# A pair of up blocks by Strassen's scheme: seven quarter products for eight in two feed-forward stages

## The chip, the cores and the metric

The kernel runs on one core of one Trainium2 chip. The metric is the time of one execution on the device in microseconds (us). Arrays are fp32; the kernel was timed in three runs, and one more execution was profiled.

## The reference

A sequence of 512 tokens of 1024 features passes through four pairs of mixer and feed-forward stage. The last two feed-forward stages are plain ones:

```python
def sqrelu_mlp(h, w1, w2):
    return jnp.square(jax.nn.relu(h @ w1)) @ w2
...
x = x + sqrelu_mlp(rms_norm_2(x, norm_ffn[i]), ffn_w1[i], ffn_w2[i]).astype(x.dtype)
```

Here `ffn_w1` is 1024 x 4096 (up) and `ffn_w2` is 4096 x 1024 (down). The change is in `h @ w1` of these two stages.

## The kernel before

**Layout.** Everything is held feature by feature: a tile has 128 features on the partitions and 512 tokens beside each other. x has 8 such tiles (`KT`), the hidden layer of a plain stage has 32 (`MLP_TILES`). All weights are one stream of blocks of 128 x 1024 words (`BLOCK`), consumed in the order of `STREAM`. An up block holds, for 128 hidden features, the 8 weight squares of 128 x 128 along the 1024 input features; a down block holds the 8 squares along the 1024 output features.

**Split in two parts.** A product of fp32 precision is made of three matmuls on rounded operands (type fp32r). Each weight block is split by ScalarE into a high part (`act_split`, L300, `wraw` to `whi`) and by VectorE into the low rest (`dve_split`, L323, `wlo` = `wraw` - `whi`). The normalised x has `hnhi` and `hnlo`, a hidden tile has `ahi` (L559) and `alo` (L564). `three` (L341 to L343) issues high x high, high x low, low x high into one PSUM bank. `wlo` lies in the same memory as `wraw`; there are four slots.

**A plain up stage.** `pe_up` takes one block after the other: 8 x 3 matmuls of 512 columns into bank m % 4; the first two are interleaved with the making of `hnhi` and `hnlo` (`pe_up_first`). The norm's factor `rstd` is computed meanwhile: squares on ScalarE (L397), added up by VectorE (L409), summed over the features by a matmul with ones (L419), then Ln and Exp on ScalarE (L361, L362). It multiplies each token's column after the product: VectorE makes relu times `rstd` (L849) into the hidden tile in `arena`, ScalarE squares it (L834). After each block `w_used` is raised; block i is loaded when block i - 4 has been used (`sp_stream`). The loops run on the engines, four blocks a trip (`tiles`).

**A plain down stage.** All 8 banks accumulate over the 32 hidden tiles; `dve_add` (L750) adds them to x as they are finished. `BANKS_FREED` gives the order in which the first tile's products go to the banks, and `MIXERS` what each bank waits for.

**Order.** Each engine runs its own list of instructions in order, and semaphores (`wait_ge`, `then_inc`) order the engines. Before the change the work of GpSimd is in other stages; in its list a load of tables waits for the first mixer of the plain part and is issued near the start of the first plain feed-forward stage.

## Time and profile before

| | |
|---|---|
| time, median of 3 runs | 2635.78 us (2635.65 to 2636.78) |
| the profiled execution's own time | 2636.36 us |
| its span in the trace | 2634.6 us |
| mean granted clock of TensorE | 1.0 (2.4 GHz) |
| TensorE busy | 2604.4 us (99%) |
| VectorE, ScalarE, GpSimd busy | 1526.8, 1178.7, 249.9 us |

The span goes from the first to the last instruction; the time of an execution has some 1.8 us around it. The duration of a matmul in the trace contains its way through the array, so matmuls overlap in time; the distance between the starts of two is what one costs in a stream. PE is TensorE, PEld its weight loads, DVE VectorE, ACT ScalarE, POOL GpSimd, SP the queue that loads the weights.

### The profile page before, as it was taken

How to read it: one execution, taken by the hardware profiler on the slowest of the kernel's cores; microseconds unless marked ns; L12 is line 12 of the kernel's file. 1: busy time of each engine (PE TensorE's matmuls, PEld its weight loads, DVE VectorE, ACT ScalarE, POOL GpSimd, SP SyncE). 2: the span in 40 equal slices, each digit the busy share in tenths (PEclk: the TensorE clock that was granted, in tenths of full speed). 3: DMA queues.
4: the chain of work that ended last, by engine and by line, in shares of the span. 5: the costliest groups of instructions: out<-in, count | busy, mean ns of one | idle time of the engine just before them, and what ended most of it. 6: DMA issues, size and time to landing. Idle time of an engine off the chain costs nothing. (4 is left out here: it accounts for less than half of the span.)

```text
span 2634.6 us, 33003 instructions
## 1 busy us (share of the span) xinstructions
PE 2604.4 (99%) x11682; PEld 2021.1 (77%) x11682; DVE 1526.8 (58%) x2136; ACT 1178.7 (45%) x1858; POOL 249.9 (9%) x204
## 2 busy tenths in 40 slices
PE   9999999999999999999999999999999999999999
PEld 7855788888786557788888776788888777888887
DVE  4466677643988785677643787543333536533333
ACT  3326544333547894444333687532333425422332
POOL 0021100000104781100000130000000002000000
PEclk9999999999999999999999999999999999999999
DMA  5310333233244442233333220233333321233332
GB/s 212 96 56 9 102 96 96 96 96 96 86 132 127 122 128 80 80 97 99 98 96 96 94 64 1 75 100 96 97 99 98 104 81 53 92 96 97 99 98 96
DMA packets 71430, 246.02 MB, mean 93 GB/s; under 512 B 7564, under 2 KB 7692, under 8 KB 70960
## 3 DMA queue, kind: packets, MB, share of 16 engines
q1 hardware_dynamic: 70256, 236.43, 28.9%
q0 software_dynamic: 944, 8.46, 0.9%
q8 instruction: 51, 0.84, 0.1%
q14 instruction: 35, 0.29, 0.0%
q10 hardware_dynamic: 144, 0.00, 0.0%
HBM read 242.63 MB, written 2.24 MB: 93 GB/s over the span
## 5 line engine op out<-in xcount | busy, mean ns | idle before, releaser
L323 DVE TENSOR_TENSOR wlo<-wraw,whi 128x1024 fp32r<-128x1024 f32 x405 | 506.4, 1251 | 574.3 <-ACT whi L300 573.5
L341 PE MATMUL bank<-hnhi,whi 128*128 128x512 f32 x1952 | 779.0, 399 | 2.0 <-DVE arena L1567 1.2
L342 PE MATMUL bank<-hnlo,whi 128*128 128x512 f32 x1952 | 760.6, 390 | 0.0
L343 PE MATMUL bank<-hnhi,wlo 128*128 128x512 f32 x1952 | 760.4, 390 | 0.0
L300 ACT ACTIVATE whi<-wraw 128x1024 fp32r<-128x1024 f32 x409 | 430.3, 1054 | 537.4 <-DMA wraw<-in_w 537.2
L341 PE MATMUL bank<-ahi,whi 128*128 128x512 f32 x1184 | 463.1, 391 | 1.0 <-DVE alo L564 0.7
L342 PE MATMUL bank<-alo,whi 128*128 128x512 f32 x1184 | 460.8, 389 | 0.0
L343 PE MATMUL bank<-ahi,wlo 128*128 128x512 f32 x1184 | 460.7, 389 | 0.0
L341 PEld LDWEIGHTS bank<-hnhi,whi 128*128 128x128 f32 x1952 | 366.4, 188 | 110.1 <-issue 34.4
L342 PEld LDWEIGHTS bank<-hnlo,whi 128*128 128x128 f32 x1952 | 366.6, 188 | 80.5 <-issue 6.5
L343 PEld LDWEIGHTS bank<-hnhi,wlo 128*128 128x128 f32 x1952 | 366.4, 188 | 77.8
L341 PEld LDWEIGHTS bank<-ahi,whi 128*128 128x128 f32 x1184 | 222.2, 188 | 51.4 <-DVE alo L564 3.8
L343 PEld LDWEIGHTS bank<-ahi,wlo 128*128 128x128 f32 x1184 | 222.2, 188 | 46.4
L342 PEld LDWEIGHTS bank<-alo,whi 128*128 128x128 f32 x1184 | 222.3, 188 | 46.1 <-issue 0.5
L785 ACT ACTIVATE mT<-mT,cols 128x512 f32<-128x512 f32 x88 | 71.8, 816 | 221.0 <-DVE mT L483 221.0
L834 ACT ACTIVATE arena<-arena (+1 forms) x64 | 40.4, 632 | 221.7 <-DVE arena L849 221.7
L559 ACT ACTIVATE ahi<-arena 128x512 fp32r (+1 forms) x140 | 88.2, 631 | 97.1 <-PE bank L343 96.4
L808 DVE SCALAR_TENSOR_TENSOR mT<-mT,cols 128x511 f32<-128x511 f32 x88 | 66.1, 751 | 97.3 <-ACT mT L785 97.3
L564 DVE TENSOR_TENSOR alo<-arena,ahi 128x512 fp32r<-128x512 f32 x140 | 96.8, 691 | 36.4 <-ACT ahi L559 34.1
L744 POOL TENSOR_TENSOR xT<-xT,mT 128x512 f32<-128x512 f32 x20 | 33.9, 1728 | 873.3 <-DVE mT L736 873.3
L483 DVE TENSOR_TENSOR arena<-bank,rstd 128x512 f32<-128x512 f32 (+3 forms) x48 | 36.6, 765 | 116.0 <-PE bank L343 104.5
L849 DVE SCALAR_TENSOR_TENSOR arena<-bank,rstd 128x512 f32 (+1 forms) x64 | 44.1, 691 | 102.9 <-PE bank L343 96.4
(306 smaller groups left out, 2511.1 us busy)
## 6 DMA issues: line engine op xcount, KB each, us to landing
wraw<-in_w SPq DMA_DIRECT2D x410, 512.0 KB, 3.6
arena<-cs_scratch SPq DMA_DIRECT2D x20, 512.0 KB, 6.0
over_a<-cs_scratch SPq DMA_DIRECT2D x12, 512.0 KB, 6.0
arena<-in_rpb POOLq DMA_DIRECT2D x1, 2880.0 KB, 14.2
out_dram<-xT SPq DMA_DIRECT2D x8, 256.0 KB, 2.0
arena<-in_t_step POOLq DMA_DIRECT2D x2, 897.0 KB, 4.8
arena<-in_t_ab POOLq DMA_DIRECT2D x1, 1536.0 KB, 6.8
xT<-in_x SPq DMA_DIRECT2D x2, 512.0 KB, 5.9
```

What stands on the lines that cost most here:

```text
L300: act.activation(whi[:, slot * BLOCK:(slot + 1) * BLOCK], wraw[:, slot * BLOCK:(slot + 1) * BLOCK], ACT.Copy).then_inc(sem("w_hi"), 1)
L323: dve.tensor_tensor(wlo[:, slot * BLOCK:(slot + 1) * BLOCK], wraw[:, slot * BLOCK:(slot + 1) * BLOCK], whi[:, slot * BLOCK:(slot + 1) * BL ...
L341: pe.matmul(out, wh, ah, start=start, stop=False)
L342: pe.matmul(out, wh, al, start=False, stop=False)
L343: return pe.matmul(out, wl, ah, start=False, stop=stop)
L483: dve.tensor_tensor(out, src, by, ALU.mult).then_inc(sem(done), 1)
L559: act.activation(ahi[:, c:c + SEQ], src(k), ACT.Copy).then_inc(sem("a_hi"), 1)
L564: dve.tensor_tensor(alo[:, c:c + SEQ], MIXERS[name][0](k), ahi[:, c:c + SEQ], ALU.subtract).then_inc(sem("a_lo"), 1)
L785: act.activation(cbuf(m), ubuf(m), ACT.Identity, bias=col("fb", m + 44 * f), scale=col("fw", m + (132 * f + 44))).then_inc(sem("ffn_center ...
L808: dve.scalar_tensor_tensor(out=c[:, 1:SEQ], in0=u[:, 0:SEQ - 1], scalar=col("fw", m + 132 * f), in1=c[:, 1:SEQ], op0=ALU.mult, op1=ALU.add ...
L834: act.activation(tile(m), tile(m), ACT.Square).then_inc(sem("mlp_hidden"), 1)
L849: dve.scalar_tensor_tensor(out=tile(m), in0=bank[m.base % 4][:, :], scalar=0.0, in1=rstd[:, :], op0=ALU.max, op1=ALU.mult).then_inc(sem("m ...
```

## The change

In both plain stages blocks 0 to 7 stay as they were (their order written out, no loop). From block 8 on two blocks are one product: 256 hidden features x 1024 inputs x 512 tokens, cut in half each way, is a 2 x 2 product of quarters. It is done with seven quarter products (Winograd's form of Strassen's scheme) with 15 sums in place of eight products:

- Weights: a11, a12 are the two halves of the first block's inputs, a21, a22 of the second's. GpSimd makes s1 = a21 + a22, s2 = s1 - a11, s3 = a11 - a21, s4 = a12 - s2, each 128 x 512. ScalarE and VectorE split each of a11, s1, a12, s2, a22, s3, s4 in high and low (`high`, `low`): seven pieces of 512 columns where two of 1024 were.
- Tokens: t1 to t4 are sums of quarters of the normalised x (inputs in halves, tokens in halves). They are made once per stage, during blocks 0 to 7, by GpSimd (t1) and VectorE (t2, t3, t4), with high and low parts (`tok_hi`, `tok_lo`).
- Products: each is 4 x 3 matmuls of 256 columns (`product`). Three banks per pair, x, w and z, two pairs in turn. x starts with a11; ScalarE copies x to z (`copy_z`); a12 is added to x, s2 and then s3 to z. w takes s1; ScalarE copies it to SBUF (`copy_w`), VectorE writes w = z + copy (`sum_w`) before s3 and s4 are added, and after s3 writes the fourth quarter z + copy to the hidden tile (`sum_c`); a22 is then added to z. VectorE makes relu times `rstd` in four pieces of 256 columns.
- TensorE's order in cycle n: a11(n), s3(n-1), s4(n-1), s1(n), a22(n-1), a12(n), s2(n). The products of a pair run over two cycles.
- The high parts have one place each in `whi` (a22 has two), the low parts one each. A load of a block of pair n + 2 waits for the split of a12(n) and for s4(n).
- The load of tables on GpSimd's queue moves behind the first stage's pairs; the first down product visits banks 6 and 7 first.

```diff
+PAIRS = (MLP_TILES - PLAIN) // 2
+QUARTER = 4 * P
 WIDE = 897
 NEG = -1e30
...
 
+        def extra(b):
+
+            return 5 * PAIRS * sum(b >= FIRST[f"mlp_down{f}"] for f in range(2))
...
             rows = FIRST["c_in"] + 17
-            for lo, hi in ((4, rows), (rows, Z0 + 5), (Z0 + 5, Z0 + 18), (Z0 + 18, NBLOCKS)):
...
                         sp_rows(sp, i.base - lo)
+            for f in range(2):
+                sp_pairs(sp, f)
+                rest = FIRST[f"mlp_down{f}"] + 4
+                for i in tiles(sp, rest, NBLOCKS if f else FIRST["mlp_up1"] + PLAIN + 4):
+                    sp.wait_ge(sem("w_used"), i.value(1, extra(rest) - 3))
...
             slot = i.base % 4
-            dve.wait_ge(sem("w_hi"), i.value(1, 1))
...
+        USED = pair_counts([s for c in range(PAIRS + 1) for s in before(
+            ("a11", c), ("s3", c - 1), ("s4", c - 1), ("s1", c), ("a22", c - 1), ("a12", c), ("s2", c))])
+        SPLIT = pair_counts(before(("a11", 0), ("s1", 0), ("a12", 0), ("s2", 0), ("a22", 0)) + [
+            s for c in range(PAIRS) for s in before(("a11", c + 1), ("s3", c), ("s4", c), ("s1", c + 1), ("a22", c + 1),
+                                                    ("a12", c + 1), ("s2", c + 1))])
...
+        def quarter_hi(f, q, n):
+
+            freed, half = {"a11": (4, 0), "s1": (4, 1), "a12": (5, 0), "s2": (5, 1), "s3": (6, 0), "s4": (6, 1),
+                           "a22": (7, n % 2)}[q]
+            a = (FIRST[f"mlp_up{f}"] + freed) % 4 * BLOCK + half * QUARTER
+            return whi[:, a:a + QUARTER]
...
+        def sp_pairs(sp, f):
+
+            for i in range(first_pair(f) + 4, FIRST[f"mlp_down{f}"] + 4):
+                n = (i - first_pair(f)) // 2 - 2
+                sp.wait_ge(sem("w_lo"), split(f, "a12" if n else "a22", n))
+                sp.wait_ge(sem("sum_pool"), pool_summed(f, "s4", n))
+                sp_load(sp, At(i))
+
+        def pool_pairs(pool, f):
...
+            for n in range(PAIRS):
+                wait_block(pool, f, n, 0)
+                wait_block(pool, f, n, 1)
+                if n:
+                    pool.wait_ge(sem("w_lo"), split(f, "s1", n - 1))
+                pool.tensor_tensor(sum_raw("s1"), block_raw(f, n, "a21"), block_raw(f, n, "a22"), ALU.add)\
+                    .then_inc(sem("sum_pool"), 1)
+                if n:
+                    pool.wait_ge(sem("w_lo"), split(f, "s2", n - 1))
+                pool.wait_ge(sem("sum_pool"), pool_summed(f, "s1", n))
+                pool.tensor_tensor(sum_raw("s2"), sum_raw("s1"), block_raw(f, n, "a11"), ALU.subtract)\
+                    .then_inc(sem("sum_pool"), 1)
+                if n:
+                    pool.wait_ge(sem("w_lo"), split(f, "s3", n - 1))
+                pool.tensor_tensor(sum_raw("s3"), block_raw(f, n, "a11"), block_raw(f, n, "a21"), ALU.subtract)\
+                    .then_inc(sem("sum_pool"), 1)
+                if n:
+                    pool.wait_ge(sem("w_lo"), split(f, "s4", n - 1))
+                pool.wait_ge(sem("sum_pool"), pool_summed(f, "s2", n))
+                pool.tensor_tensor(sum_raw("s4"), block_raw(f, n, "a12"), sum_raw("s2"), ALU.subtract)\
+                    .then_inc(sem("sum_pool"), 1)
+
...
+            def high(q, n):
+
+                if n == 0 or (q, n) == ("a22", 1):
+                    act.wait_ge(sem("w_used"), plain_used(f, {"a11": 4, "s1": 4, "a12": 5, "s2": 5, "s3": 6, "s4": 6, "a22": 7}[q]))
+                else:
+                    act.wait_ge(sem("w_used"), used(f, q, n - 2 if q == "a22" else n - 1))
+                if q in SUM_AT:
+                    act.wait_ge(sem("sum_pool"), pool_summed(f, q, n))
+                    src = sum_raw(q)
+                else:
+                    wait_block(act, f, n, q == "a22")
+                    src = block_raw(f, n, q)
+                act.activation(quarter_hi(f, q, n), src, ACT.Copy).then_inc(sem("w_hi"), 1)
+
+            def copy_z(n):
+                act.wait_ge(sem("w_used"), used(f, "a11", n))
+                if n == 0:
+                    act.wait_ge(sem("mlp_relu"), relu_done(f, 6))
+                if n >= 2:
+                    act.wait_ge(sem("mlp_relu"), relu_done(f, PLAIN + 2 * (n - 2) + 1))
+                act.activation(pair_bank(n, "z"), pair_bank(n, "x"), ACT.Copy).then_inc(sem("sum_copied"), 1)
+
+            def copy_w(n):
+                act.wait_ge(sem("w_used"), used(f, "s1", n))
+                if n >= 2:
+                    act.wait_ge(sem("sum_dve"), c_summed(f, n - 2))
+                act.activation(w_copy(n), pair_bank(n, "w"), ACT.Copy).then_inc(sem("sum_copied"), 1)
...
+                    for j in range(KT):
+                        act_square(act, j)
+                    act_split(act, At(FIRST[name] + 3))
+                    for j in range(4):
+                        ins = act.activation(over_a[:, j * SEQ:(j + 1) * SEQ], xt(j), ACT.Copy, scale=col(g, g0 + j))
+                    ins.then_inc(sem("sum_copied"), 1)
+                    act_norm_rstd(act, norm)
+                elif m <= 5:
...
+            for n in range(PAIRS):
+                copy_z(n)
+                if n == 0:
+                    high("a22", 0)
+                if n + 1 < PAIRS:
+                    high("a11", n + 1)
+                high("s3", n)
+                high("s4", n)
+                copy_w(n)
+                if n + 1 < PAIRS:
+                    high("s1", n + 1)
+                if n:
+                    hidden_square(PLAIN + 2 * (n - 1))
+                if n + 1 < PAIRS:
+                    high("a22", n + 1)
+                    high("a12", n + 1)
+                if n:
+                    hidden_square(PLAIN + 2 * (n - 1) + 1)
+                if n + 1 < PAIRS:
+                    high("s2", n + 1)
+            act.wait_ge(sem("w_used"), used(f, "s1", PAIRS - 1))
+            act_split(act, At(FIRST[f"mlp_down{f}"]))
+            act.wait_ge(sem("w_lo"), split(f, "s4", PAIRS - 1))
+            act_high(act, f"mlp_down{f}", At(0))
+            act_high(act, f"mlp_down{f}", At(1))
+            act.wait_ge(sem("w_used"), used(f, "s2", PAIRS - 1))
+            act_split(act, At(FIRST[f"mlp_down{f}"] + 1))
+            hidden_square(MLP_TILES - 2)
+            hidden_square(MLP_TILES - 1)
+            act.wait_ge(sem("w_used"), used(f, "a22", PAIRS - 1))
+
...
+            def low(q, n):
+                dve.wait_ge(sem("w_hi"), split(f, q, n))
+                src = sum_raw(q) if q in SUM_AT else block_raw(f, n, q)
+                dve.tensor_tensor(quarter_low(q, n), src, quarter_hi(f, q, n), ALU.subtract).then_inc(sem("w_lo"), 1)
+
+            def sum_w(n):
+                dve.wait_ge(sem("w_used"), used(f, "s2", n))
+                dve.wait_ge(sem("sum_copied"), w_copied(f, n))
+                dve.tensor_tensor(pair_bank(n, "w"), pair_bank(n, "z"), w_copy(n), ALU.add).then_inc(sem("sum_dve"), 1)
+
+            def sum_c(n):
+                dve.wait_ge(sem("w_used"), used(f, "s3", n))
+                dve.tensor_tensor(pair_tile(n, 1, 1), pair_bank(n, "z"), w_copy(n), ALU.add).then_inc(sem("sum_dve"), 1)
+
+            def relu_z(n):
+                dve.wait_ge(sem("sum_dve"), c_summed(f, n))
+                relu(pair_tile(n, 1, 1), pair_tile(n, 1, 1), 1)
+                dve.wait_ge(sem("w_used"), used(f, "s4", n))
+                relu(pair_tile(n, 0, 1), pair_bank(n, "w"), 1).then_inc(sem("mlp_relu"), 1)
...
+            for n in range(PAIRS):
+                if n:
+                    sum_w(n - 1)
+                else:
+                    low("a22", 0)
+                if n + 1 < PAIRS:
+                    low("a11", n + 1)
+                if n:
+                    sum_c(n - 1)
+                low("s3", n)
+                if n:
+                    relu_z(n - 1)
+                low("s4", n)
+                if n + 1 < PAIRS:
+                    low("s1", n + 1)
+                if n:
+                    dve.wait_ge(sem("w_used"), used(f, "a22", n - 1))
+                    relu(pair_tile(n - 1, 1, 0), pair_bank(n - 1, "z"), 0).then_inc(sem("mlp_relu"), 1)
+                if n + 1 < PAIRS:
+                    low("a22", n + 1)
+                dve.wait_ge(sem("w_used"), used(f, "a12", n))
+                relu(pair_tile(n, 0, 0), pair_bank(n, "x"), 0)
+                if n + 1 < PAIRS:
+                    low("a12", n + 1)
+                    low("s2", n + 1)
+            dve_split(dve, At(FIRST[f"mlp_down{f}"]))
+            dve_low_part(dve, f"mlp_down{f}", At(0))
+            sum_w(PAIRS - 1)
+            dve_low_part(dve, f"mlp_down{f}", At(1))
+            sum_c(PAIRS - 1)
+            dve_split(dve, At(FIRST[f"mlp_down{f}"] + 1))
+            relu_z(PAIRS - 1)
+            dve.wait_ge(sem("w_used"), used(f, "a22", PAIRS - 1))
+            relu(pair_tile(PAIRS - 1, 1, 0), pair_bank(PAIRS - 1, "z"), 0).then_inc(sem("mlp_relu"), 1)
+
...
+            def product(q, n, c, start=False):
+
+                pe.wait_ge(sem("w_lo"), split(f, q, n))
+                out, hi, lo = pair_bank(n, c), quarter_hi(f, q, n), quarter_low(q, n)
+                t = {"s1": "t1", "s2": "t2", "s3": "t3", "a22": "t4"}.get(q)
+                if t and n == 0:
+                    pe.wait_ge(sem("sum_dve"), token_low(f, t))
+                for j in range(4):
+                    if t:
+                        ah, al = tok_hi[:, token(t, j)], tok_lo[:, token(t, j)]
                     else:
+                        half = slice(HALF_N, SEQ) if q == "s4" else slice(0, HALF_N)
+                        ah, al = (a[:, half] for a in hn_parts(j if q == "a11" else 4 + j))
+                    wh, wl = hi[:, j * P:(j + 1) * P], lo[:, j * P:(j + 1) * P]
+                    if start:
+                        mm = three(pe, out, (wh, wl), (ah, al), j == 0, j == 3)
                     else:
+                        pe.matmul(out, wh, ah, start=False, stop=False, skip_group_check=True)
+                        pe.matmul(out, wh, al, start=False, stop=False, skip_group_check=True)
+                        mm = pe.matmul(out, wl, ah, start=False, stop=j == 3, skip_group_check=True)
+                mm.then_inc(sem("w_used"), 1)
+
+            for n in range(PAIRS + 1):
+                if n < PAIRS:
+                    pe.wait_ge(sem("mlp_relu"), relu_done(f, (4, 7)[n] if n < 2 else PLAIN + 2 * (n - 2)))
+                    product("a11", n, "x", True)
+                if n:
+                    pe.wait_ge(sem("sum_dve"), w_summed(f, n - 1))
+                    product("s3", n - 1, "z")
+                    product("s4", n - 1, "w")
+                if n < PAIRS:
+                    if n == 0:
+                        pe.wait_ge(sem("mlp_relu"), relu_done(f, 5))
+                    product("s1", n, "w", True)
+                if n:
+                    pe.wait_ge(sem("sum_dve"), c_summed(f, n - 1))
+                    product("a22", n - 1, "z")
+                if n < PAIRS:
+                    pe.wait_ge(sem("sum_copied"), z_copied(f, n))
...
+        def pair_banks(total):
+            def free(pe, m):
+                if m < 6:
+                    pe.wait_ge(sem("mlp_relu"), total - {0: 2, 1: 2, 2: 2, 3: 1, 4: 1, 5: 0}[m])
+            return free
+
...
                 .then_inc(sem("tables_loaded"), 16)
             pool_mla(pool)
-            pool.wait_ge(sem("x_ready"), 40)
+            pool_pairs(pool, 0)
+            pool.wait_ge(sem("w_used"), used(0, "a22", PAIRS - 1))
             pool.dma_start(arena[:, ML_T["stepF"]:ML_T["stepF"] + TABLE_WORDS["step"]], A["t_step"])\
                 .then_inc(sem("tables_loaded"), 16)
             pool_ml(pool)
+            pool_pairs(pool, 1)
```

## Rows read from the trace of the kernel before

**Rows 1.** The page's header and busy times of the engines.
```profile
span 2634.6 us, 33003 instructions
PE 2604.4 (99%) x11682; PEld 2021.1 (77%) x11682; DVE 1526.8 (58%) x2136; ACT 1178.7 (45%) x1858; POOL 249.9 (9%) x204
```

**Rows 2.** Stretches: plain blocks 0 to 7, then the rest of each up stage.
```profile
core 0: us, PE busy (x) PEld busy (x) DVE busy (x) ACT busy (x) POOL busy (x), PEclk, DMA share, GB/s
1705.00:1749.00 44.00, 44.00 (x193) 36.06 (x193) 24.09 (x30) 20.24 (x29) 0.56 (x1) 1.00 0.40 129
1750.00:1880.00 130.00, 130.00 (x575) 107.67 (x574) 47.24 (x50) 38.97 (x50) 0.00 (x0) 1.00 0.32 97
2325.00:2456.00 131.00, 131.00 (x579) 108.48 (x578) 47.24 (x50) 38.97 (x50) 0.00 (x0) 1.00 0.31 96
```

**Rows 3.** Timeline of one up block: start us, us, engine, line.
```profile
1783.11 0.69 DVE L849 SCALAR_TENSOR_TENSOR arena<-bank,rstd 128x512 f32 x1 [1.75 <-PE bank L343]
...
1783.25 0.39 PE L343 MATMUL bank<-hnhi,wlo 128*128 128x512 f32 x1
1783.26 0.19 PEld L341 LDWEIGHTS bank<-hnhi,whi 128*128 128x128 f32 x1
...
1784.46 1.04 ACT L300 ACTIVATE whi<-wraw 128x1024 fp32r<-128x1024 f32 x1
...
1785.54 1.23 DVE L323 TENSOR_TENSOR wlo<-wraw,whi 128x1024 fp32r<-128x1024 f32 x1 [1.74 <-ACT whi L300]
...
1788.55 0.69 DVE L849 SCALAR_TENSOR_TENSOR arena<-bank,rstd 128x512 f32 x1 [1.78 <-PE bank L343]
```

**Rows 4.** Timeline of TensorE: runs of short plain fp32 matmuls.
```profile
1090.87 2.32 PE L701 MATMUL bank<-base_t 128*128 128x256 f32 x10
...
2230.22 0.60 PE L2564 MATMUL bank<-arena,mT 128*128 128x128 f32 x4
```

**Rows 5.** Timeline of weight loads, whose matmuls have two columns.
```profile
1515.21 0.86 PEld L2097 LDWEIGHTS bank<-arena,over_hn 128*128 128x128 f32 x7 [0.24 <-issue]
```

**Rows 6.** Groups by shape: count, busy us, mean ns.
```profile
L564 DVE TENSOR_TENSOR alo<-arena,ahi 128x512 fp32r<-128x512 f32 x140 | 96.8, 691 | 36.4 <-ACT ahi L559 34.1
L2715 DVE SCALAR_TENSOR_TENSOR arena<-bank,arena 128x256 f32<-128x256 f32 x4 | 1.7, 417 | 0.7 <-PE bank L2589 0.7
L559 ACT ACTIVATE ahi<-arena 128x512 fp32r x88 | 55.8, 634 | 65.0 <-PE bank L343 64.4 <-DVE arena L1825 0.5
L954 ACT ACTIVATE arena<-bank 128x256 f32<-128x256 f32 x8 | 3.0, 379 | 0.2 <-PE bank L918 0.2
L701 PE MATMUL bank<-base_t 128*128 128x256 f32 x40 | 9.3, 379 | 0.0
L2564 PE MATMUL bank<-arena,mT 128*128 128x128 f32 x16 | 2.4, 274 | 0.0
L1646 POOL TENSOR_TENSOR mT<-arena 128x512 f32<-128x512 f32 x40 | 50.4, 1287 | 68.9 <-DVE arena L1560 64.9 <-DMA arena<-cs_scratch 2.0 <-issue 1.9
```

**Rows 7.** Timeline: GpSimd beside VectorE, VectorE alone, the last matmul.
```profile
1464.76 6.78 POOL L744 TENSOR_TENSOR xT<-xT,mT 128x512 f32<-128x512 f32 x4 [359.20 <-DVE mT L736]
...
1465.85 1.12 DVE L402 SCALAR_TENSOR_TENSOR hnlo<-xT,cols,hnhi 128x512 fp32r<-128x512 f32 x1
...
2277.82 0.69 DVE L750 TENSOR_TENSOR xT<-xT,bank 128x512 f32<-128x512 f32 x1
2278.43 0.75 DVE L402 SCALAR_TENSOR_TENSOR hnlo<-xT,cols,hnhi 128x512 fp32r<-128x512 f32 x1
...
2630.74 1.36 DVE L750 TENSOR_TENSOR xT<-xT,bank 128x512 f32<-128x512 f32 x2
...
2631.00 0.39 PE L343 MATMUL bank<-ahi,wlo 128*128 128x512 f32 x1
```

**Rows 8.** Timeline: TensorE restarts after a wait for VectorE.
```profile
2230.42 0.69 DVE L2702 TENSOR_TENSOR arena<-bank,rstd 128x512 f32<-128x512 f32 x1 [2.52 <-PE bank L343]
...
2231.22 0.19 PEld L341 LDWEIGHTS bank<-hnhi,whi 128*128 128x128 f32 x1 [0.37 <-issue]
...
2231.26 0.47 PE L341 MATMUL bank<-hnhi,whi 128*128 128x512 f32 x1 [0.21 <-DVE arena L2702]
2231.56 0.40 PE L342 MATMUL bank<-hnlo,whi 128*128 128x512 f32 x1
...
2232.26 0.39 PE L342 MATMUL bank<-hnlo,whi 128*128 128x512 f32 x1
```

**Rows 9.** DMA issues with us to landing, and ScalarE's wait for the norm sum.
```profile
wraw<-in_w SPq DMA_DIRECT2D x410, 512.0 KB, 3.6
arena<-in_t_step POOLq DMA_DIRECT2D x2, 897.0 KB, 4.8
...
L361 ACT ACTIVATE rstd<-bank,stats 128x512 f32<-128x512 f32 x1 | 0.7, 690 | 5.5 <-PE bank L419 5.5
```

More of the change, by code:

```diff
@@ L48 @@
 MLP_TILES = 4 * DM // P
+PLAIN = 8
+PAIRS = (MLP_TILES - PLAIN) // 2
+QUARTER = 4 * P
 WIDE = 897
@@ L273, in sp_stream @@
             rows = FIRST["c_in"] + 17
-            for lo, hi in ((4, rows), (rows, Z0 + 5), (Z0 + 5, Z0 + 18), (Z0 + 18, NBLOCKS)):
+            for lo, hi in ((4, rows), (rows, Z0 + 5), (Z0 + 5, Z0 + 18), (Z0 + 18, FIRST["mlp_up0"] + PLAIN + 4)):
                 if lo == rows:
@@ L852, in pe_mlp_up, with pair_counts, before @@
-        def pe_mlp_up(pe, f, norm):
-            pe_up(pe, f"mlp_up{f}", norm, [(2, 4, None, 0), (4, 32, "mlp_relu", 32 * f - 3)])
+        def pair_counts(order):
+            return {q: i + 1 for i, q in enumerate(order)}
+        def before(*steps):
+            return [(q, n) for q, n in steps if 0 <= n < PAIRS]
+        USED = pair_counts([s for c in range(PAIRS + 1) for s in before(
+            ("a11", c), ("s3", c - 1), ("s4", c - 1), ("s1", c), ("a22", c - 1), ("a12", c), ("s2", c))])
@@ new lines, in quarter_low, with pair_bank, pair_tile, w_copy @@
+        def quarter_low(q, n):
+            if q == "a22" and n % 2:
+                return odd_lo[:, :]
+            a = ("a11", "s1", "a12", "s2", "s3", "s4", "a22").index(q) * QUARTER
+            return quarter_lo[:, a:a + QUARTER]
+        def pair_bank(n, c):
+            return bank[3 * (n % 2) + "xwz".index(c)][:, 0:HALF_N]
+        def pair_tile(n, second, half):
+            return tile(PLAIN + 2 * n + second)[:, half * HALF_N:(half + 1) * HALF_N]
+        def w_copy(n):
+            return sq[:, n % 2 * HALF_N:(n % 2 + 1) * HALF_N]
```

185 lines of the change are left out of this document (149 added, 36 removed).

## The prediction

> **What bounds the kernel now.** I read the page's busy shares first: TensorE is busy for 99% of the span, VectorE for 58%, ScalarE for 45%, GpSimd for 9% [rows 1]. The table of stretches says the same of both feed-forward up stages: TensorE 130 us in 130 us at the full granted clock, VectorE 36%, ScalarE 30%, GpSimd idle [rows 2]. So the time of an up block is its column work. In the timeline the same VectorE instruction (L849, one per block) starts at 1783.11 and 1788.55 [rows 3], and a block has 8 x 3 products: 5.44/24 = 0.2267 us from one 128x512 product to the next. Each has a weight load of 0.19 us beside it [rows 3]. At 2.4 GHz 512 columns are 0.2133 us, so 0.0133 us is something else; on it the change hangs.
>
> **What the change does to TensorE.** Blocks 8 to 31 of a stage become 12 pairs, in two stages 24 pairs. A pair was 48 products of 512 columns, 48 x 0.2267 = 10.88 us; 24 pairs are 261.1 us. It becomes 7 quarter products of 4 x 3 = 12 matmuls of 256 columns: 84 matmuls, with 84 weight loads where there were 48. The columns streamed fall by an eighth, weight loads rise by three quarters. Break-even for the bare stream is 10.88/84 = 0.1295 us per matmul.
>
> No row shows a 256-column matmul on data rounded for one pass. The nearest are:
> - Plain fp32 matmuls take twice as long per column: ten of 256 columns take 2.32 us in all with one lasting 0.379, so (2.32 - 0.38)/9 = 0.216 apart; four of 128 columns with weights of their own are (0.60 - 0.27)/3 = 0.110 apart (runs [rows 4], one matmul's duration [rows 6]). The second streams as long as our case (0.1067 us), with a new 128x128 weight load each. So load and stream do overlap at this length: lower bound 0.110.
> - Two-column matmuls show the bare cost of loads: seven in 0.86 us, (0.86 - 0.19)/6 = 0.112 [rows 5].
> - The 0.0133 us over the columns is either per matmul, giving 0.1067 + 0.0133 = 0.120, or per column (a sixteenth), giving 0.1133. For plain fp32 the surplus is some 0.0025 at 128 and 256 columns alike [rows 4], thus per matmul.
> - From above: bare load plus surplus, 0.112 + 0.013 = 0.125; and, if the slower steps after a restart (2231.56 to 2232.26 in three steps, 0.233 each [rows 8]) never ended, 0.1067 + 0.020 = 0.127.
>
> I take 0.120, since the only surplus seen at two lengths is per matmul. 2016 matmuls are 241.9 us: 19.2 below 261.1. The ends are 0.110 (221.8) and 0.127 (256.0).
>
> The Trainium skill (TensorE: Matmul & The Clock Gate, Back-to-back issue gap) says that in a stream of weight loads and matmuls both set the spacing, and gives 81 ns at 128 columns against 56 without loads, which speaks against this change. An estimate from that page, 0.025 us on top of 0.109, would be 0.134 and 2016 x 0.134 = 270 us; rows 4 show no such surplus for plain fp32.
>
> **The wait that the new order puts in.** TensorE goes a11(n+1), s3(n), s4(n), s1(n+1), a22(n), a12(n+1), s2(n+1). s3(n) waits for `sum_w(n)`, which needs s2(n), the product just before a11(n+1); so one quarter product, 12 x 0.120 = 1.44 us, covers it. But VectorE's list has `low("s2", n+1)` ahead of `sum_w(n)`, and that waits for ScalarE's `high("s2", n+1)`, which waits for s2(n) to leave its single place in `whi`. From the time at which a11(n+1) issues:
> - last matmul of s2(n) drains: modelled duration less pitch, 0.389 - 0.227 = 0.16; the waiting engine starts 0.02 after (matmul over at 2631.39, the second of the two L750 begins at 2632.10 - 0.69 = 2631.41) [rows 7]: 0.18
> - high, 128x512 copy by ScalarE: 0.63; handover 0.04 (L300 ends at 1785.50, L323 starts at 1785.54) [rows 3, 6]
> - low, 128x512 by VectorE: 0.69; sum_w, 256 columns with a PSUM operand: 0.42, starting some 0.08 before the one ahead is over, as L750 and L402 do (2278.43 - 2277.82 = 0.61 for 0.69), so 0.34 [rows 6, 7]
> - VectorE to TensorE: L2702 ends at 2231.11, the load starts at 2231.22, its matmul at 2231.26 and lasts 0.47 for 0.39: 0.11 + 0.04 + 0.08 = 0.23 [rows 8].
>
> 0.18 + 0.63 + 0.04 + 0.69 + 0.34 + 0.23 = 2.11 us. TensorE stands 2.11 - 1.44 = 0.67 us per cycle. Cycles 2 to 11 in two stages: 20 x 0.67 = 13.4 us. A steady cycle is 72 matmuls plus 2.11, 10.75 us for 10.88 before: the drop in columns pays for this wait and hardly more.
>
> **The two ends.** First cycle: the second weight block of pair 1 is issued as plain block 7 ends and lands 3.6 us later [rows 9]; then GpSimd's s1 and s2 at 1.28 each (the rows' solo value [rows 6]), high 0.63, low 0.69, sum_w 0.42 and handovers 0.3: 8.3 us, against 5 quarter products, 7.2: 1.1 us, twice. Last cycle: no a11 covers s3(11), and VectorE first does `dve_split` and `dve_low_part` of the down stage, 1.23 + 0.69 [rows 3, 6], after a12(11)'s relu of 0.42: done 2.5 us after a12 ends, with s2 lasting 1.44: 1.06 + 0.42 + 0.16 = 1.64 us, twice. Of the down stage only the first matmuls are moved; their first two banks (6 and 7) wait for nothing, and the others come 1.4 us and more later, after the last relus.
>
> **What lies beside.** Per pair VectorE has 7 lows at 0.69 and 6 operations of 256 columns at 0.42, 7.3 us; ScalarE 7 highs at 0.63, 2 PSUM copies at 0.38 and 2 squares at 0.63, 6.4; GpSimd 4 sums at 1.28, 5.1 [rows 6]. In 10.75 us all fit. I followed the order through one cycle: a12's high, the square and s2's high need 1.3 of the 1.44 us that s2 lasts, VectorE reaches `low("s2")` some 0.3 us early. The other waits of TensorE (`sum_c` for a22, `copy_z` for a12) have two or more products as cover. Weight loads of later pairs wait for GpSimd's s4 and a12's low, come some 0.5 us into the cycle before and are used after 8.8 us. In the plain blocks the work on tokens (4 ScalarE copies of 512, 4 roundings of 1024 columns, 12 VectorE instructions of 256, 4 of 1024, GpSimd's t1) adds 6.7 us to ScalarE's 20.2 and 9.9 to VectorE's 24.1 in a stretch of 44 us; the 2.5 us of copies ahead of `rstd` fall into ScalarE's wait of 5.5 us for the norm sum [rows 2, 9]; uncovered they would cost 2.5 us per stage, but bank 0 is next needed only at block 4. The table load on GpSimd's queue, moved behind the pairs, lands in 4.8 us [rows 9], and its tables are needed only by the mixer after the down stage of 32 x 5.44 = 174 us: nothing.
>
> GpSimd's sums read SBUF while VectorE's lows read two operands there. Where both ran, VectorE's L402 took 1.12 for 0.75 and GpSimd's sums 1.7 (four in 6.78 us) for 1.28 [rows 6, 7]. Per pair 10.3 us of such work share 10.75. `low("s2")` falls between GpSimd's s1(n+2) and s2(n+2), and slack of 0.3 us absorbs one collision of 0.4 nearly; I take nothing, and 0.4 x 20 = 8 us as the upper bound. The Trainium skill (SBUF — State Buffer, Who interferes with whom) says the later of the two blocks until the first ends. By that rule a low can be late by a whole sum; L402's 0.37 is well below that, so the trace agrees on the conflict and not on its size.
>
> **Sum.** 241.9 + 13.4 + 2.2 + 3.3 = 260.8 against 261.1: -0.3 us on the profiled execution's 2636.36 (span 2634.6 and 1.8 around it). That execution lies 0.6 above the median 2635.78, so on the median 2635.5 us.
>
> **Rivals.**
> 1. The surplus is per column or vanishes (0.110 to 0.115). At 0.1133: 228.4; cover 1.36, wait 0.75 x 20 = 15.0; ends 5.7: 249.1, 12 us less, 2624. At 0.110: 221.8 + 15.8 + 5.9 = 243.5, 2618. For it: 0.0133/0.2133 is exactly a sixteenth. Against: the fp32 rows.
> 2. The other side: weight loads, now as long as the stream, slow it. It decides above 0.123. At 0.125: 252.0 + 0.61 x 20 + 5.2 = 269.4, 2644; at 0.127: 256.0 + 0.59 x 20 + 5.1 = 272.9, 2648. For it: load floor 0.112 against a stream of 0.107. Against: 0.110 at 128 fp32 columns.
> 3. The shared SBUF reads of VectorE and GpSimd lengthen the chain by 0.4 per cycle: 2643.5.
> 4. Loads and matmuls do not overlap for rounded data: 0.107 + 0.112 = 0.219, 2016 x 0.219 = 441.5, over 2800. The 0.19 us loads in 0.227 us steps speak against it.
>
> **Chances.** Forecast (0.117 to 0.123, wait as above) 0.30; rival 1 0.34; rival 2 0.24; rival 3 0.09; rival 4 0.03. They spread: I can't tell fixed from proportional surplus by the trace. 0.2% or 5.3 us is about what a measurement of this kernel can tell from no change. Faster 0.35, same 0.30, slower 0.35. The range runs from 0.110 to 0.125 with one collision of 0.4 in every cycle (2644 + 8): 2619 to 2652; the likeliest case's own is 2630 to 2641.
>
> **What would show it.** In the changed profile: the step from one 256-column matmul to the next (0.120); TensorE idle once per pair ahead of the first matmul of s3, released by VectorE's `sum_w`, 0.67 us; 10.75 us from one pair's a11 to the next; VectorE about 68% busy there and its lows at 0.69 or up to 1.1. The prediction is wrong if the step is not 0.120 (each nanosecond is 1.8 us), if the wait before s3 is absent, or if TensorE waits at other products, for GpSimd or a weight block.

## The result

The changed kernel takes 2653.46 us (median of 4, 2653.11 to 2654.83), the kernel before beside it 2636.28 (4 runs, 2635.65 to 2637.04): a ratio of 1.0065, 95% interval 1.0054 to 1.0077. It is slower by 17 us and lies above the range of 2619 to 2652. The span went from 2634.6 [rows 1] to 2653.0 us. The page of the changed kernel, its header and busy times:

```profile
span 2653.0 us, 35180 instructions
PE 2595.4 (98%) x12546; PEld 2052.5 (77%) x12546; DVE 1684.5 (63%) x2384; ACT 1257.7 (47%) x2042; POOL 387.4 (15%) x302
```

TensorE is busy for 9 us less in a span that is 18 us longer, so it waits more than was forecast. The table of stretches shows where (its columns as in [rows 2]; the first two rows are the first wait and what follows it, the last two the two pair stretches):

```profile
1757.60:1763.90 6.30, 0.34 (x4) 0.14 (x2) 6.30 (x8) 1.26 (x3) 5.07 (x4) 0.88 0.07 16
1763.90:1768.00 4.10, 4.10 (x19) 4.10 (x20) 2.40 (x3) 0.63 (x1) 0.93 (x1) 0.50 0.66 251
1768.00:1876.00 108.00, 101.86 (x825) 99.83 (x825) 92.62 (x128) 58.93 (x108) 50.37 (x38) 0.99 0.26 92
1750.60:1890.40 139.80, 126.24 (x1009) 123.81 (x1008) 115.99 (x158) 72.15 (x132) 59.50 (x44) 0.98 0.26 95
2336.00:2475.00 139.00, 125.44 (x1008) 123.01 (x1008) 116.34 (x158) 72.20 (x132) 59.71 (x44) 0.98 0.27 96
```

A pair stretch (first matmul of the first pair to first matmul of the down stage) was 12 x 10.88 = 130.6 us; it is now 139.9 in the first stage and 139.2 in the second, 18.0 us more in all, of the 18.4 us by which the spans differ. The other 0.4 us lie ahead of the first stage. VectorE is busy for 116 of 140 us there, 83% where the prediction said 68%. In the first row VectorE is busy for all 6.30 us and TensorE for 0.34; in the second the granted clock is 0.50.

One line of the table of waits holds what is new in TensorE's waiting (engine and line waited for: us in all, times, longest):

```profile
PE bank L1201 <- DVE bank L1110: 27.1, 24, 6.0
```

L1110 is `sum_w`. So the place was forecast, once per pair ahead of s3; the size was not. TensorE's timeline has the wait in the first cycle and what follows it, and the wait in a steady cycle with the stream on both sides:

```profile
1757.64 0.28 PE L360 MATMUL bank<-hnhi,quarter_lo 128*128 128x256 f32 x1
1763.88 0.58 PE L1201 MATMUL bank<-tok_hi,whi 128*128 128x256 f32 x1 [5.96 <-DVE bank L1110]
1764.26 0.42 PE L1202 MATMUL bank<-tok_lo,whi 128*128 128x256 f32 x1
1764.47 0.41 PE L1203 MATMUL bank<-tok_hi,quarter_lo 128*128 128x256 f32 x1
...
1768.95 0.40 PE L1203 MATMUL bank<-hnhi,quarter_lo 128*128 128x256 f32 x1
...
1786.83 0.28 PE L359 MATMUL bank<-hnlo,whi 128*128 128x256 f32 x1
1786.95 0.28 PE L360 MATMUL bank<-hnhi,quarter_lo 128*128 128x256 f32 x1
1787.91 0.39 PE L1201 MATMUL bank<-tok_hi,whi 128*128 128x256 f32 x1 [0.68 <-DVE bank L1110]
1788.13 0.28 PE L1202 MATMUL bank<-tok_lo,whi 128*128 128x256 f32 x1
1788.25 0.29 PE L1203 MATMUL bank<-tok_hi,quarter_lo 128*128 128x256 f32 x1
```

The step from one matmul to the next is 0.12 us, as forecast. The distance over a steady wait is 1787.91 - 1786.95 = 0.96, over the first 1763.88 - 1757.64 = 6.24. After the first the steps are (1768.95 - 1764.26)/22 = 0.213 us, which is 256 columns at 1.2 GHz.

Why `sum_w` is late is in VectorE's and GpSimd's timelines of the same cycle. VectorE:

```profile
1782.44 1.51 DVE L1105 TENSOR_TENSOR quarter_lo<-over_a,whi 128x512 fp32r<-128x512 f32 x1 [0.42 <-ACT whi L997]
1783.88 0.41 DVE L1075 SCALAR_TENSOR_TENSOR arena<-bank,rstd 128x256 f32<-128x256 f32 x1
1784.21 1.76 DVE L1105 TENSOR_TENSOR odd_lo<-wraw,whi 128x512 fp32r<-128x512 f32 x1
1785.90 0.41 DVE L1075 SCALAR_TENSOR_TENSOR arena<-bank,rstd 128x256 f32<-128x256 f32 x1
1786.23 0.68 DVE L1105 TENSOR_TENSOR quarter_lo<-wraw,whi 128x512 fp32r<-128x512 f32 x1
1786.83 0.68 DVE L1105 TENSOR_TENSOR quarter_lo<-over_a,whi 128x512 fp32r<-128x512 f32 x1
1787.43 0.42 DVE L1110 TENSOR_TENSOR bank<-bank,sq 128x256 f32<-128x256 f32 x1
```

GpSimd and, below it, ScalarE's high part of s2 (L997) in that cycle:

```profile
1782.10 1.30 POOL L967 TENSOR_TENSOR over_a<-wraw,over_a 128x512 f32<-128x512 f32 x1 [0.63 <-DVE quarter_lo L1105]
1784.13 1.30 POOL L953 TENSOR_TENSOR over_a<-wraw 128x512 f32<-128x512 f32 x1 [0.72 <-DVE quarter_lo L1105]
...
1785.83 0.63 ACT L997 ACTIVATE whi<-over_a 128x512 fp32r<-128x512 f32 x1 [0.28 <-PE bank L1203]
```

The low of a22 (`odd_lo`) begins at 1784.21, 0.08 after GpSimd's sum, and is over at 1785.97, 0.54 after the sum's end at 1785.43: it takes 1.76 us for 0.69 [rows 6]. ScalarE hands over s2's high part at 1786.46; VectorE, which should have stood waiting for it, begins the low at 1786.83, 0.33 us late (0.04 is the handover). That is 0.96 instead of 0.63. The relus, with one operand in a PSUM bank, keep their 0.41 beside the same sums.

This is not one unlucky row. In the trace of the changed kernel 91 of the 168 lows begin while a GpSimd sum is under way, between 0.03 and 1.08 us after its start, and all 91 end 0.54 to 0.55 us after the end of that sum. The 75 lows that meet no sum take 0.67 to 0.69 us. So a low that meets a sum waits for the sum's end, and its length tells only how early in the sum it began.

In the first cycle the same happens to a whole row of lows. VectorE, then GpSimd:

```profile
1753.14 1.29 DVE L1105 TENSOR_TENSOR quarter_lo<-wraw,whi 128x512 fp32r<-128x512 f32 x2 [0.48 <-ACT whi L997]
1754.35 5.19 DVE L1105 TENSOR_TENSOR quarter_lo<-over_a,whi 128x512 fp32r<-128x512 f32 x3
1759.46 1.75 DVE L1105 TENSOR_TENSOR odd_lo<-wraw,whi 128x512 fp32r<-128x512 f32 x1
1761.13 0.41 DVE L1075 SCALAR_TENSOR_TENSOR arena<-bank,rstd 128x256 f32<-128x256 f32 x1
1761.46 1.41 DVE L1105 TENSOR_TENSOR quarter_lo<-wraw,whi 128x512 fp32r<-128x512 f32 x1
1762.80 0.68 DVE L1105 TENSOR_TENSOR quarter_lo<-over_a,whi 128x512 fp32r<-128x512 f32 x1
1763.40 0.42 DVE L1110 TENSOR_TENSOR bank<-bank,sq 128x256 f32<-128x256 f32 x1
```

```profile
1754.31 1.29 POOL L953 TENSOR_TENSOR over_a<-wraw 128x512 f32<-128x512 f32 x1 [4.69 <-DMA wraw<-in_w]
1755.75 1.56 POOL L958 TENSOR_TENSOR over_a<-over_a,wraw 128x512 f32<-128x512 f32 x1
1757.28 1.71 POOL L962 TENSOR_TENSOR over_a<-wraw 128x512 f32<-128x512 f32 x1
1758.95 1.71 POOL L967 TENSOR_TENSOR over_a<-wraw,over_a 128x512 f32<-128x512 f32 x1
1760.62 1.71 POOL L953 TENSOR_TENSOR over_a<-wraw 128x512 f32<-128x512 f32 x1
```

The weight block of pair 1 lands, and GpSimd runs five sums one behind the other. VectorE is never idle from 1753.14 to `sum_w` at 1763.40. From 1754.35 on it works through six lows and one relu in 9.05 us; alone they would take 6 x 0.61 + 0.34 = 4.0, counted from start to start. The longest of these lows takes 1.81 us.

### The profile page after: what moved, and what is told of

Same layout as the page of the kernel before. It is cut to its first block and busy times, and to the rows that moved or that the text cites. A ratio compares the mean times of both kernels' runs of the same rounds, so it can differ in the third digit from the quotient of the medians.

```text
span 2653.0 us, 35180 instructions
## 1 busy us (share of the span) xinstructions
PE 2595.4 (98%) x12546; PEld 2052.5 (77%) x12546; DVE 1684.5 (63%) x2384; ACT 1257.7 (47%) x2042; POOL 387.4 (15%) x302
## 5 line engine op out<-in xcount | busy, mean ns | idle before, releaser
L340 DVE TENSOR_TENSOR wlo<-wraw,whi 128x1024 fp32r<-128x1024 f32 x357 | 447.0, 1254 | 436.9 <-ACT whi L317 435.9
L358 PE MATMUL bank<-hnhi,whi 128*128 128x512 f32 (+1 forms) x1664 | 656.8, 395 | 2.0 <-DVE arena L1938 1.2
L359 PE MATMUL bank<-hnlo,whi 128*128 128x512 f32 (+1 forms) x1664 | 638.4, 384 | 0.0
L360 PE MATMUL bank<-hnhi,wlo 128*128 128x512 f32 x1568 | 611.1, 390 | 0.0
L317 ACT ACTIVATE whi<-wraw 128x1024 fp32r<-128x1024 f32 x361 | 380.0, 1055 | 479.7 <-DMA wraw<-in_w 479.4
L358 PEld LDWEIGHTS bank<-hnhi,whi 128*128 128x128 f32 x1664 | 312.8, 188 | 95.0 <-issue 34.5
L359 PEld LDWEIGHTS bank<-hnlo,whi 128*128 128x128 f32 x1664 | 313.0, 188 | 65.9 <-issue 6.5
L360 PEld LDWEIGHTS bank<-hnhi,wlo 128*128 128x128 f32 x1568 | 294.4, 188 | 62.7
L761 POOL TENSOR_TENSOR xT<-xT,mT 128x512 f32<-128x512 f32 x20 | 33.9, 1730 | 873.3 <-DVE mT L753 873.3
L1105 DVE TENSOR_TENSOR quarter_lo<-over_a,whi 128x512 fp32r<-128x512 f32 x96 | 99.9, 1044 | 19.1 <-ACT whi L997 17.5
L1201 PE MATMUL bank<-tok_hi,whi 128*128 128x256 f32 x288 | 85.1, 296 | 27.1 <-DVE bank L1110 27.1
```

The lines of the kernel that those rows point to most:

```text
L317: act.activation(whi[:, slot * BLOCK:(slot + 1) * BLOCK], wraw[:, slot * BLOCK:(slot + 1) * BLOCK], ACT.Copy).then_inc(sem("w_hi"), 1)
L340: dve.tensor_tensor(wlo[:, slot * BLOCK:(slot + 1) * BLOCK], wraw[:, slot * BLOCK:(slot + 1) * BLOCK], whi[:, slot * BLOCK:(slot + 1) * BL ...
L358: pe.matmul(out, wh, ah, start=start, stop=False)
L359: pe.matmul(out, wh, al, start=False, stop=False)
L360: return pe.matmul(out, wl, ah, start=False, stop=stop)
L1105: dve.tensor_tensor(quarter_low(q, n), src, quarter_hi(f, q, n), ALU.subtract).then_inc(sem("w_lo"), 1)
```

## The experiments

Eleven kernels ran, in three rounds and on two chips; all ratios are to the kernel before on the same chip and in the same round (2636.65 to 2637.03 us). Where a distance is given, it is from TensorE's last matmul before the wait to the first behind it. Theory: collisions of VectorE's lows with GpSimd's sums. Rivals: the order of `low("s2")` and `sum_w` alone, or something that the step of the matmul hides.

**1. Order: `sum_w(n)` ahead of `low("s2", n + 1)`.**

```diff
-                if n:
-                    sum_w(n - 1)
-                else:
+                if n == 0:
                     low("a22", 0)
...
                 if n + 1 < PAIRS:
                     low("a12", n + 1)
+                    sum_w(n)
                     low("s2", n + 1)
```

> The changed kernel with one swap on VectorE: sum_w(n) ahead of low of s2(n+1). Theory A (the order of VectorE's list makes the wait before s3): in the steady cycles TensorE's wait before s3 vanishes, because drain, sum_w and handover are some 0.8 us against 1.44 us of cover. 16 waits of 0.95 and 4 of 0.62 us go, 17.6 us, and 0.6 us in each first cycle: 2635 us, from 2653.5. The long wait in each first cycle stays, at some 5.6 us. Theory B (VectorE is late because its lows collide with GpSimd's sums, whatever the order): the waits move to other products and the time stays above 2642 us.

Measured: 2644.07 us (2642.47 to 2645.24), ratio 1.0026 (1.0016 to 1.0036). It gives back 9.4 of the 17 us and no more. The table counts the wait for `sum_w` 12 times in place of 24 (between those stand distances of some 0.36), and the mean of VectorE's lows (the group by shape below it: count, busy us, mean ns) is no better:

```profile
PE bank L1200 <- DVE bank L1110: 16.5, 12, 5.3
```

```profile
L1105 DVE TENSOR_TENSOR quarter_lo<-over_a,whi 128x512 fp32r<-128x512 f32 x96 | 104.2, 1088 | 11.8 <-ACT whi L997 9.8
```

`sum_w` no longer waits for s2's high and low, so what remains is VectorE's backlog: in the steady cycle before the wait at 1786.22 it has no idle time from 1777.90 to the end of `sum_w` at 1786.17.

**2. GpSimd's sums cut to 8 of 512 columns.** This run leaves the weight sums out but for 8 columns; all else is done. The first of the four edits:

```diff
-                pool.tensor_tensor(sum_raw("s1"), block_raw(f, n, "a21"), block_raw(f, n, "a22"), ALU.add)\
+                pool.tensor_tensor(sum_raw("s1")[:, 0:8], block_raw(f, n, "a21")[:, 0:8], block_raw(f, n, "a22")[:, 0:8], ALU.add)\
```

> The changed kernel, GpSimd's four weight sums of each pair cut to 8 of 512 columns, all waits and semaphores kept (the sums are left out but for these columns). Theory B: VectorE's lows fall from a mean of about 1.04 us to 0.69, TensorE's wait in each first cycle from 6.2 us to about 1.4 us (the excess of eight lows, 4.9 us, is gone), the clock does not fall after it, and the steady waits of 0.95 become 0.62 us: 2653.5 - 9.6 - 3.5 - 5.3 = 2635 us. If the lows are long for another reason (reading over_a, or ScalarE's copies beside them), nothing moves: 2653 us.

Measured: 2635.71 us (2634.3 to 2636.3), ratio 0.9995 (0.9986 to 1.0004). The groups by shape and the wait:

```profile
L1105 DVE TENSOR_TENSOR quarter_lo<-over_a,whi 128x512 fp32r<-128x512 f32 x96 | 66.1, 692 | 43.5 <-ACT whi L997 41.8
L1105 DVE TENSOR_TENSOR odd_lo<-wraw,whi 128x512 fp32r<-128x512 f32 x12 | 8.3, 691 | 1.4
```

```profile
PE bank L1201 <- DVE bank L1110: 11.7, 24, 1.5
```

The lows are back at 0.69 (1.04 and 1.58 in the changed kernel). All steady distances are 0.63, the first 1.16, the last 1.74. A pair stretch is 129.85 us, twice 259.7; the prediction's sum was 260.8. So without collisions the sum holds.

**3. Both edits.** Like the last, it leaves out the sums but for 8 columns.

> Swap and 8 columns together (the weight sums are left out but for 8 columns). If order and collisions are all that the change loses, what is left is the stream at 0.120 us per matmul, a first cycle with at most 1.4 us of wait and a last one with 1.7: 2636.3 - 19.2 + 2 to 6 = 2619 to 2623 us. If weight loads or a third wait cost as well: above 2627 us.

Measured: 2622.23 us (2620.94 to 2623.01), ratio 0.9944 (0.9930 to 0.9957). Only the first and the last wait are left (distances of 0.55 and 1.74), and a stretch is 123.2 us; 1008 x 0.120 = 121.0 is the stream. With neither cost the scheme is 14.8 us below the kernel before. The run also shows what each of the two causes costs alone: 13.5 us the order (run 2 less run 3), 21.8 us the sums (run 1 less run 3). Together they cost 31.2, so they overlap by 4.

**4. The ends, with whole sums:** run 1, with `sum_w(0)` right after `low("s3", 0)`, `sum_c(0)` after `low("s1", 1)`, and the last `sum_w` ahead of the down stage's split. The part of the edit at the end:

```diff
+            sum_w(PAIRS - 1)
             dve_split(dve, At(FIRST[f"mlp_down{f}"]))
             dve_low_part(dve, f"mlp_down{f}", At(0))
-            sum_w(PAIRS - 1)
```

> The changed kernel with full work and VectorE's list reordered: sum_w(n) ahead of low of s2(n+1), in the first cycle sum_w(0) right after low of s3(0) and sum_c(0) after low of s1(1), in the last cycle sum_w ahead of the split of the down block. Theory A plus backlog: steady waits gone (17.6 us), the first wait of 6.4 us falls to under 2 us in pieces, with it the half-clock stretch (1.8 us each), the last one from 1.7 to 0.9: 2618 to 2626 us, faster than the kernel before the change. Theory B: VectorE's work is behind anyway, each wait comes back at the next product, 2635 us or more.

Measured: 2637.78 us (2637.08 to 2639.33), ratio 1.0004 (0.9995 to 1.0013). The last distance fell from 1.74 to 0.81. The first wait is gone at s3(0) and back at s3(1), with a distance of 4.24 for the 5.62 of run 1:

```profile
1767.14 0.28 PE L360 MATMUL bank<-hnhi,quarter_lo 128*128 128x256 f32 x1
1771.38 0.53 PE L1205 MATMUL bank<-tok_hi,whi 128*128 128x256 f32 x1 [3.96 <-DVE bank L1110]
```

VectorE's backlog isn't made smaller by another order of its list; what can be put off is due one cycle later.

**5. The sums in pieces, all of the work done.** If a low is late by what is left of the GpSimd instruction that is under way, shorter instructions bound that. If only the amount of shared reading counts, they don't. This tells the mechanism, since GpSimd has no less to do. The edit for two pieces, with the first of its four uses (four pieces have `QUARTER // 4`):

```diff
+            def summed(out, a, b, op):
+                for c in range(0, QUARTER, QUARTER // 2):
+                    part = slice(c, c + QUARTER // 2)
+                    ins = pool.tensor_tensor(out[:, part], a[:, part], b[:, part], op)
+                ins.then_inc(sem("sum_pool"), 1)
...
-                pool.tensor_tensor(sum_raw("s1"), block_raw(f, n, "a21"), block_raw(f, n, "a22"), ALU.add)\
-                    .then_inc(sem("sum_pool"), 1)
+                summed(sum_raw("s1"), block_raw(f, n, "a21"), block_raw(f, n, "a22"), ALU.add)
```

In four pieces, in the order of the changed kernel:

> The changed kernel with each of GpSimd's weight sums cut into four instructions of 128 columns; all the work is done. Theory (a VectorE low is late by what is left of the GpSimd instruction that is under way, up to a whole sum): the lateness is bounded by a piece, some 0.4 us in place of up to 1.06, so the lows' mean falls from 1.04 to 0.8 or 0.9, the first wait before s3 from 6.2 to some 3 us, the steady wait from 0.96 to the 0.63 that the run without sums showed: 2653.5 - 2 x 3.2 - 16 x 0.33 = some 2642 us. Rival (the two share the reads in proportion, and only the amount of shared work counts): the lows stay at 1.04, GpSimd pays some start-up for each piece, and the time stays at 2653 or rises.

Measured: 2645.06 us (2644.21 to 2646.21), ratio 1.0032 (1.0020 to 1.0044). The first distance fell from 6.24 to 3.92, the steady ones to between 0.63 and 0.91: 8.4 us of the 11.5 that the theory gave.

In four pieces, with `sum_w` ahead (run 1):

> The kernel with sum_w ahead of the low part of s2, with the sums in four pieces as well; all the work is done. It took 2644.1 with whole sums and 2622.2 with sums of 8 columns. Theory: the first wait of 5.6 falls to some 2.5 us and the steady waits of 0.36 and 0.64 to 0.1 to 0.3: some 2632 us. Rival (proportional sharing): 2644 or more.

Measured: 2635.42 us (2633.61 to 2637.47), ratio 0.9996 (0.9987 to 1.0005). The first distance is 3.03; in the first stage steady ones of 0.49 to 0.76 stay, in the second there are none.

In two pieces, with `sum_w` ahead:

> As the run with sum_w ahead and sums in four, with two pieces of 256 columns. Theory: lateness bounded by half a sum, some 0.65 us: between the whole sums (2644) and four pieces (some 2632), some 2637 us. Rival: 2644 or more; or, if GpSimd's start-up per piece is what counts, two pieces better than four.

Measured: 2628.93 us (2627.41 to 2629.54), ratio 0.9971 (0.9960 to 0.9982): faster than the kernel before by 7.7 us. Its groups and its wait:

```profile
L1107 DVE TENSOR_TENSOR quarter_lo<-over_a,whi 128x512 fp32r<-128x512 f32 x96 | 80.6, 841 | 21.3 <-ACT whi L999 21.0
L1107 DVE TENSOR_TENSOR odd_lo<-wraw,whi 128x512 fp32r<-128x512 f32 x12 | 11.3, 943 | 0.0
L951 POOL TENSOR_TENSOR over_a<-wraw 128x256 f32<-128x256 f32 x96 | 101.4, 1076 | 78.6 <-DMA wraw<-in_w 46.6 <-DVE quarter_lo L1107 24.0 <-issue 8.0
```

```profile
PE bank L1202 <- DVE bank L1112: 8.2, 4, 2.6
```

Of 24 waits four are left, the two first (distances of 2.9) and the two last (1.74). Against run 1 the mean low fell from 1.09 to 0.84 and `odd_lo` from 1.58 to 0.94, while GpSimd's busy time rose from 391.3 to 440.3 us. The longest low is 1.82 us with whole sums, 1.25 with halves and 0.99 with quarters (runs of the swapped order). So it is not GpSimd's amount of work that delays VectorE but the length of one of its instructions: the theory holds and proportional sharing falls. The ranking was wrong, though: four pieces were to beat two, and they lose by 6.5 us, which the expectation had named only as a rival. This row of the run with four and `sum_w` ahead shows why:

```profile
L999 ACT ACTIVATE whi<-over_a 128x512 fp32r<-128x512 f32 x96 | 60.3, 631 | 80.1 <-POOL over_a L951 39.6 <-PE bank L1204 22.0 <-PE bank L360 17.4
```

The lows are better still (0.76), but a sum is now four pieces of 0.6 to 0.7 us in the profile, and ScalarE waits 39.6 us for GpSimd's sums (3.9 with two pieces, 1.5 with whole sums). Of these 33.9 us fall in the first stage, where GpSimd is busy for 115 of 131 us and sets the pace. In the second stage they are 5.6, and no steady wait of TensorE is left. Why the two stages differ is not shown.

In four pieces, with the order of run 4:

> The kernel with sum_w and sum_c of pair 0 early, sum_w ahead of low s2 in the other cycles and ahead of the down stage's split at the end (2637.8 with whole sums), with the sums in four pieces; all the work is done. Theory: the 4.2 us wait at s3(1) falls to some 1.5, the steady waits to 0.1 to 0.3: 2637.8 - 5.4 - 6 = some 2626 us, clearly below the kernel before. Rival: 2638 or more.

Measured: 2632.49 us (2630.27 to 2634.21), ratio 0.9984 (0.9975 to 0.9993). The distance at s3(1) is 3.4 us where a wait of 1.5 was expected, so 5.3 of the expected 11.4 us came.

In two pieces, in the order of the changed kernel:

> The changed kernel with each of GpSimd's weight sums cut into two instructions of 256 columns and nothing else; all the work is done. With four pieces it took 2645.1, with sum_w ahead as well two pieces (2628.9) beat four (2635.4) by 6.5 us, since GpSimd's time per sum grew from 1.3 to some 2.6 us with four pieces and to some 2.0 with two. If the two edits only add, whole sums to two pieces is worth 15.2 us as it was with sum_w ahead, 2638 us; but the wait of 0.63 in every cycle that the order of low s2 and sum_w makes stays (20 x 0.62 = 12.4 us), first wait some 3.2: 241.9 + 12.4 + 6.5 + 3.3 + clock 2 = 266 against 261 before: some 2641 us. Rival (order plays no part once the sums are in pieces): 2629.

Measured: 2644.32 us (2643.79 to 2645.62), ratio 1.0028 (1.0017 to 1.0040). All 20 steady distances are 0.63 (16 were 0.96 with whole sums), as in the run without sums; that part comes from the order alone. The first is 4.02, where I expected a wait of 3.2.

In two pieces, with `sum_w` ahead, and the last `sum_w` ahead of the down split:

> The kernel with sum_w ahead of low s2 and the sums in two pieces (2628.9), with the last sum_w of each stage also ahead of the down stage's split; all the work is done. The last wait falls from 1.74 to 0.81 as in the run with early sums, nothing else moves: 2 x 0.93 = 1.9 us less, 2627.0. Rival (the down stage's first products then wait for their split instead): 2629 or more.

Measured: 2628.73 us (2624.48 to 2631.82), ratio 0.9969 (0.9958 to 0.9979). The runs spread over 7 us, and the median is the same as without the edit. The profiled executions say more. The one of this kernel (2624.48) has the last distance at 0.80, as expected, and full granted clock in both pair stretches, which take 124.6 us each. The one without the edit (2628.77) has 125.5 and 127.0. Of these 3.4 us 1.9 are the last waits, as forecast, and the rest is a half clock behind one of the first waits. So the edit is worth its 1.9 us, and what blurs the medians is the clock.

In two pieces, with the order of run 4:

> The kernel with all the moved sums (2637.8 with whole sums, 2632.5 with four pieces), with two pieces; all the work is done. Theory: steady waits nothing, last wait 0.81, the wait of 3.4 to 4.2 at s3(1) falls below 2 since VectorE's lows are 0.85 and GpSimd's sums 2.0: 2628.9 - 1.9 - 2 x 1.5 = some 2624 us. Rival (VectorE's backlog in the first two cycles only moves from s3(0) to s3(1)): 2627 or more.

Measured: 2627.92 us (2626.44 to 2632.45), ratio 0.9968 (0.9956 to 0.9981). The distance at s3(1) is 3.1 us: the rival (the backlog only moves) is right here, and the 1 us below the simple swap is within the spread.

## Why the prediction was wrong

The terms, on the two pair stretches together. "Measured" is the distance between matmul starts less the 0.12 of a step, with what the first step behind the wait is longer (0.10, since 1787.91 to 1788.13 is 0.22; in the first cycle 0.26, since 1763.88 to 1764.26 is 0.38):

| term | forecast | measured |
|---|---|---|
| stream of 2016 matmuls | 241.9 | 241.9 |
| first cycle, 2 waits | 2.2 | 12.7 |
| half clock behind them | 0 | 3.5 (the rest to the sum) |
| cycles 2 to 11, 20 waits | 13.4 | 17.5 |
| last cycle, 2 waits | 3.3 | 3.4 |
| sum | 260.8 | 279.1 |

- **The step of a 256-column matmul: right.** 0.120 us. The surplus of 0.0133 over the columns is there at 512 and at 256 columns alike, so it is fixed per matmul. Rival 1 (per column), rival 2 (weight loads slow it) and rival 4 (no overlap) fall: a load alone was 0.112 in [rows 5], and the step is still columns plus 0.0133.
- **The wait before s3 and its chain: right but for collisions.** Forecast 0.67; with the lows at 0.69 it is 0.63 - 0.12 + 0.10 = 0.61 (in the run without sums, and with two pieces in the order of the changed kernel).
- **The failed step: "slack of 0.3 us absorbs one collision of 0.4 nearly; I take nothing, and 0.4 x 20 = 8 us as the upper bound".** The size of a collision was read from L402 [rows 7], 0.37 us. VectorE's lows took up to 1.81 for 0.69, 1.12 more, and several in one cycle. In 16 of the 20 steady cycles 0.33 us of it came through to TensorE, 5.3 us, of which 1.2 were made good by the wait of 0.61 for 0.67; rival 3 had priced 8. The larger part, 14 us in the first cycles with the half clock behind them, lay where no rival looked.
- **How the row was misread.** GpSimd's sum beside that L402, in the trace of the kernel before:

```profile
1464.76 1.66 POOL L744 TENSOR_TENSOR xT<-xT,mT 128x512 f32<-128x512 f32 x1 [359.20 <-DVE mT L736]
```

L402 began at 1465.85, 1.09 us into this sum, and ended at 1466.97, 0.55 after the sum's end at 1466.42. That is the same 0.55 as in all 91 lows of the changed kernel. The 0.37 us was small because L402 began late in the sum, not because a collision is small. The prediction's "10.3 us of such work share 10.75" was the warning: 7 lows of 0.69 and 4 sums of 1.28 are 9.95 us of them, and if they exclude each other, a cycle is nearly full and has no slack that absorbs one.

- **The first cycle: the number was 1.1, the path was not.** (Its terms add up to 8.2 us, not 8.3, which would make it 1.0.) I followed the weight block through GpSimd and ScalarE, and didn't count what VectorE had in its list at that moment. Without collisions the distance is 1.16, near the 1.1, but in that run too VectorE is never idle from 1753.46 to the end of `sum_w`. It was already full there. That run even lacks the 2 x 1.28 us of GpSimd that the forecast counts, so that the two numbers agree is luck. Five back-to-back sums then cost 5.1 us per stage, and the half clock behind the wait of 6 us a further 2.1 us in the first stage and 1.4 in the second.
- **The last cycle: right.** 1.64 forecast, 1.72 measured.
- **The upper end.** 2652 allowed for a slower step and for collisions of 0.4, together. The bound from one row with a partial overlap was no bound. The Trainium skill (SBUF — State Buffer, Who interferes with whom) calls the contention for the port pair that VectorE and GpSimd share an exclusive lock; the prediction set that against the L402 row and chose the row. The trace of the changed kernel agrees with the lock: a low begun 0.08 us behind a 1.30 us sum ended 0.54 us after it, 1.07 us late. A low late by up to a whole sum would have been the upper bound.

What stays open: whether another start of pair 1's sums would take more off the first cycle, since every version with all the work kept a distance of 2.9 us or more at s3(0) or s3(1); and what decides whether the clock falls behind such a wait. The spread of the last two kernels follows the clock: of the eight executions of the one with the last `sum_w` moved, 2624.48 us has a mean granted clock of 1.000, 2625.19 and 2627.53 have 0.999, 2628.45 and 2629.01 have 0.998, and 2629.89 to 2631.82 have 0.997. In the profiled executions of the changed kernel and of the nine runs that do all the work, half clock followed all ten first waits with a distance of 3.9 us or more and five of the ten with 2.9 to 3.4. Six of the traces, that of the changed kernel among them, also have a stretch of half clock near 1657 us, ahead of the first plain stage, and in them the first pair starts some 1 us later. So a difference of 1 or 2 us between two kernels here can be the clock alone.

## What to carry to other kernels

Where two engines share reads, take the bound of a collision from the longest instruction of the other engine, not from the length of one row that happened to overlap; compare the two ends instead. And look for the place where several come in a row: a late load can release them all at once. Count what the list of the releasing engine holds at the moment of the chain, not only the chain itself. Where GpSimd works beside VectorE, halving its instructions was worth 9 us alone and 15 us with the order mended; quartering them lost part of it to GpSimd's own time per instruction and to its waits for VectorE. And a saving in columns is only cashed if the operations around it are ordered so that the engine that gained stays fed: the same seven products, with all the work done, gave 2653, 2644, 2635 or 2629 us.
